# Unread products on TensorE in five waits of a two-block model kernel

## The chip, the core and the metric

The kernel runs on one core of a Trainium2 chip. The core has a matrix engine (TensorE, PE in the profile, with its weight loads as PEld), three engines for elementwise work (VectorE, DVE; ScalarE, ACT; GpSimd, POOL) and an engine that only issues transfers here (SyncE, SP). Each works through its own list of instructions in order; they meet by semaphores. The metric is the device time of one execution of the whole kernel in microseconds, median of several runs; lower is better.

## The reference

The kernel computes two blocks for one sequence of 256 tokens of width 1024, all in float32. The first block mixes by a gated delta rule and by dilated attention and has a layer of experts picked by product keys; the second is conditioned on a vector `c`, has a layer of sparse attention (NSA) and a layer of a gated linear recurrence, each followed by a mixture of experts. Only these parts are touched by the change:

```python
def gated_delta_rule(q, k, v, g, beta):          # chunks of tokens, 4 heads, 2 directions
    gcum = jnp.cumsum(g.reshape(r, n, c), axis=-1)
    decay = jnp.where(lower, jnp.exp(jnp.where(lower, diff, 0.0)), 0.0)
    kb = k * beta[..., None]
    lmat = jnp.where(strict, jnp.einsum('rnid,rnjd->rnij', kb, k) * decay, 0.0)
    amat = jnp.eye(c, dtype=jnp.float32) + lmat
    sol = lax.linalg.triangular_solve(amat, rhs, left_side=True, lower=True, unit_diagonal=True)
    ...
def deltanet_branch(q, k, v, z, a, b, conv_w, a_log, dt_bias, out_norm):
    ...
    o = rmsnorm(o, out_norm) * jax.nn.silu(z.reshape(bsz, s, DN_HEADS, DN_DV).astype(f32))
    ...
def nsa_mixer(h, rel_bias, w_in, q_gain, k_gain, cmp_pe, cmp_w1, cmp_w2, w_out):
    q, kc, vc, ks, vs, kw, vw, gl = jnp.split(h @ w_in, cuts, axis=-1)
    kc = rms_norm(compress_blocks(kc.reshape(kvs), cmp_pe[0], cmp_w1[0], cmp_w2[0]), k_gain[0])
    ...
        lg = jnp.einsum('bqgrd,bngd->bgrqn', q_b, kc) * scale + bias_tbl[:, :, t5_bucket_2(dist_c)]
        p_c = masked_softmax(lg, dist_c >= 0)          # compressed keys
        ...                                            # selected keys, window: p_s, p_w
        o = gate_b[..., 0:1] * o_c + gate_b[..., 1:2] * o_s + gate_b[..., 2:3] * o_w
```

## The kernel before

The program is a row of stages. Each opens its own tiles and semaphores, gives every engine a list of instructions written by hand, and ends with a barrier of all engines. A product of f32 operands appears in the trace as two records, a transpose as one.

`idle_products` (L133) issues n matmuls of the identity (128x128) with 512 columns of constants into a PSUM bank that nobody reads. The kernel has it in `norm_stage`, ahead of and behind the transposes (L499, L508), and in the mixture of experts (L2726, L2731).

`deltanet` (L907) treats four groups (two directions, two halves of the tokens) of four heads each. TensorE sums the gates and spreads them over rows (L1097 to L1100), transposes k and then v in four steps (L1101 to L1108), each of which VectorE copies out (L1002), and makes three groups of grams for each of the four groups (L1112 to L1123). Between them stand three blocks of `work`, an object of class `Conditioning` (L292), which multiplies a slice of the second block's conditioning matrix from the ring of weights by the vector (L334) while other engines are busy. VectorE turns the grams into a masked matrix in five steps (L1009 to L1017). Then a blocked triangular inverse runs in seven levels: GpSimd masks a block (L1084, and at the first level subtracts it from the identity, L1087), TensorE transposes or multiplies (`first`, L1129; `second`, L1145), ScalarE and VectorE copy and subtract. GpSimd's mask for step i waits for TensorE's product of step i-2, as two buffers alternate.

`head_norm_gate_turn` (L1200) is the next stage: TensorE does two or three blocks of conditioning, then eight transposes (L1251), VectorE copies them out (L1240), and the stage ends. The projection behind it (`project`, L524) takes its weights from the ring of three slots: the first block's products are plain f32 (L583), the later blocks are split in two parts by VectorE (L141, L146) and multiplied in three passes (L152 to L154).

`nsa_prepare` (L2045) transposes the inputs of the compression (L2195), does three slots of conditioning (`work.tensor(pe)`, behind L2200), of which the first is turned into columns once ScalarE has copied its row (L370, then L323), and then runs 64 records of compression products (L2209), which wait for the last row (`work.moved`, 3). ScalarE copies the first row only after its squares and root of the stage.

`nsa_attention` (L2228) flips the gates with a matrix that VectorE makes at the stage's start (L2356, L2451), scores the compressed keys in two groups (`c_score`: L2387, then the bias, L2392), scores the first two pairs of heads (`score`, L2413), turns the compressed probabilities (`c_turn`, L2401) once VectorE has shifted, and ScalarE and VectorE have scaled them, and then loops over 16 pairs: turn the probabilities (L2426), score the pair after next, multiply by the values (L2439, L2446). VectorE's row maximum of a pair is L2347.

## Time and profile before

| | us |
|---|---|
| median of 3 runs | 2287.07 |
| lowest and highest | 2286.28 and 2289.59 |
| the profiled execution: its time | 2286.01 |
| the profiled execution: span from first to last instruction | 2284.2 |

| engine | busy us | share of the span |
|---|---|---|
| TensorE | 2028.8 | 89% |
| VectorE | 1379.6 | 60% |
| ScalarE | 618.4 | 27% |
| GpSimd | 547.4 | 24% |

The mean granted clock of TensorE over the span is 0.975 of full speed. The clock has two levels here, 1.00 (2.4 GHz) and 0.50 (1.2 GHz); a value between them is a stretch with both. Ends of matmuls are modelled, and successive records overlap, so the pace of a group is read from the distance of starts rather than from the length of one record.

### The profile page before, as it was taken

Reading aid. Unit: us, or ns where it says so; the run is one execution under the profiler, and the core shown is the slowest. Engines: PE = TensorE matmul, PEld = TensorE weight load, DVE = VectorE, ACT = ScalarE, POOL = GpSimd, SP = SyncE. Lnnn points to the kernel's source line nnn. Section 1 sums busy time; section 2 is a strip of 40 time slices with the busy share of each in tenths; the row PEclk is TensorE's granted clock in tenths of the full one; section 3 lists DMA queues with packets and bytes.
Section 4 is the critical chain, followed back from the end, with each engine's and each line's share of the span. In section 5 each row is a group of like instructions: output and inputs, shape, how many; then the busy total and the mean of one; then the engine's idle time right before and its main releaser. Section 6 shows DMA issues by size and latency. Waiting matters only on the chain. (4 is left out here: it accounts for less than half of the span.)

```text
span 2284.2 us, 27579 instructions
## 1 busy us (share of the span) xinstructions
PE 2028.8 (89%) x10581; PEld 1341.9 (59%) x10581; DVE 1379.6 (60%) x2493; ACT 618.4 (27%) x1050; POOL 547.4 (24%) x499
## 2 busy tenths in 40 slices
PE   8889998997997777777779888999999979899998
PEld 7678897774542222222237765666775966566684
DVE  7255564557888888655665466433666764533494
ACT  2311103422111111000020262333652151433472
POOL 1032000104443333444320182000104252100000
PEclk9799999999999999999999799999999999999999
DMA  6830655639999999999965502998996533799897
GB/s 211 310 119 1 223 202 172 221 109 420 391 421 422 421 421 422 421 420 417 421 267 183 157 2 84 375 356 350 394 375 241 187 125 119 271 361 358 351 399 281
DMA packets 142431, 650.91 MB, mean 285 GB/s; under 512 B 17975, under 2 KB 22735, under 8 KB 97083
## 3 DMA queue, kind: packets, MB, share of 16 engines
q1 hardware_dynamic: 94012, 354.03, 41.1%
q0 software_dynamic: 46336, 291.93, 31.3%
q10 hardware_dynamic: 1952, 3.18, 0.4%
q8 instruction: 85, 1.39, 0.2%
q14 instruction: 46, 0.38, 0.0%
HBM read 642.40 MB, written 16.85 MB: 289 GB/s over the span
## 5 line engine op out<-in xcount | busy, mean ns | idle before, releaser
L1872 PE MATMUL psum<-peer_uv_rows,peer_weight_diagonal 128*128 128x512 f32 x932 | 453.5, 615 | 108.4 <-DVE peer_weight_diagonal L1998 108.0
L1872 PEld LDWEIGHTS psum<-peer_uv_rows,peer_weight_diagonal 128*128 128x128 f32 x932 | 161.7, 190 | 391.1 <-DVE peer_weight_diagonal L1998 266.2
L2005 DVE SCALAR_TENSOR_TENSOR peer_uv_rows<-peer_uv_rows,peer_x 128x1024 f32<-128x1024 f32 x233 | 285.6, 1226 | 145.4 <-DMA peer_uv_rows<-peer_uv,peer_index 143.2
L1826 POOL DMA_INDIRECT peer_uv_rows<-peer_uv,peer_index x233 | 241.7, 1037 | 446.9 <-PE psum L1872 330.2
L146 DVE TENSOR_TENSOR moe_weight_parts<-weight_ring,moe_weight_parts 128x2048 fp32r<-128x2048 f32 x80 | 182.6, 2291 | 155.0 <-ACT moe_weight_parts L2925 154.6
L1905 ACT ACTIVATE peer_gelu<-peer_dots 128x1 f32<-128x1 f32 x256 | 51.5, 202 | 552.1 <-DVE peer_uv_rows L2005 500.8
L2925 ACT ACTIVATE moe_weight_parts<-weight_ring 128x2048 fp32r<-128x2048 f32 x80 | 152.1, 1911 | 35.6 <-DMA weight_ring<-moe_w 24.4
L152 PE MATMUL psum<-moe_weight_parts,moe_block_x_parts 128*128 128x512 f32 x352 | 142.4, 404 | 10.5 <-DVE moe_weight_parts L146 5.7
L3044 POOL DMA_INDIRECT h_t<-moe_tokens,moe_block_tokens x30 | 34.8, 1159 | 450.6 <-PE psum L2743 410.0
L153 PE MATMUL psum<-moe_weight_parts,moe_block_x_parts 128*128 128x512 f32 x352 | 139.1, 395 | 0.0
L154 PE MATMUL psum<-moe_weight_parts,moe_block_x_parts 128*128 128x512 f32 x352 | 138.9, 395 | 0.0
L146 DVE TENSOR_TENSOR project_weight_parts<-weight_ring,project_weight_parts 128x2048 fp32r<-128x2048 f32 (+2 forms) x52 | 120.3, 2314 | 1.8
L2809 PE MATMUL psum<-weight_ring,moe_pair_x 128*64 128x512 f32 x384 | 117.7, 600 | 0.0
L141 DVE CAST project_weight_parts<-weight_ring 128x2048 fp32r<-128x2048 f32 (+2 forms) x52 | 68.6, 1319 | 50.0 <-PEq L574 31.2
L152 PE MATMUL psum<-project_weight_parts,project_x_parts 128*128 128x512 f32 (+2 forms) x256 | 97.4, 380 | 0.0
L154 PE MATMUL psum<-project_weight_parts,project_x_parts 128*128 128x512 f32 (+2 forms) x256 | 96.5, 377 | 0.0
L153 PE MATMUL psum<-project_weight_parts,project_x_parts 128*128 128x512 f32 (+2 forms) x256 | 96.5, 377 | 0.0
L152 PE MATMUL psum<-project_x_parts,project_weight_parts 128*128 128x256 f32 x320 | 91.1, 285 | 0.0
L154 PE MATMUL psum<-project_x_parts,project_weight_parts 128*128 128x256 f32 x320 | 90.5, 283 | 0.0
L153 PE MATMUL psum<-project_x_parts,project_weight_parts 128*128 128x256 f32 x320 | 90.5, 283 | 0.0
L1998 DVE TENSOR_SCALAR peer_weight_diagonal<-constants,peer_gelu,peer_gates 128x128 f32<-128x128 f32 x256 | 87.9, 344 | 2.4 <-ACT peer_gelu L1905 2.4
L152 PEld LDWEIGHTS psum<-moe_weight_parts,moe_block_x_parts 128*128 128x128 f32 x352 | 67.1, 191 | 34.8 <-DVE moe_weight_parts L146 11.7
(574 smaller groups left out, 3882.2 us busy)
## 6 DMA issues: line engine op xcount, KB each, us to landing
weight_ring<-moe_w SPq DMA_DIRECT2D x76, 2048.0 KB, 10.3
weight_ring<-ada_w SPq DMA_DIRECT2D x24, 2048.0 KB, 9.1
moe_weight_ring_end<-moe_w SPq DMA_DIRECT2D x20, 2048.0 KB, 12.6
weight_ring<-w_in SPq DMA_DIRECT2D x17, 2048.0 KB, 9.5
weight_ring<-hgrn_w_in SPq DMA_DIRECT2D x8, 2048.0 KB, 9.7
moe_results<-moe_block_out POOLq DMA_DIRECT2D x26, 512.0 KB, 10.5
weight_ring<-nsa_w_in SPq DMA_DIRECT2D x5, 2048.0 KB, 9.0
weight_ring<-peer_wq SPq DMA_DIRECT2D x4, 2048.0 KB, 8.1
```

What stands on the lines that cost most here:

```text
L141: return nc.vector.tensor_copy(out.bitcast(F32R), x)
L146: return eng.tensor_tensor(out.bitcast(F32R), x, high, ALU.subtract)
L152: nc.tensor.matmul(out, ll, rh, start=start, stop=False)
L153: nc.tensor.matmul(out, lh, rl, start=False, stop=False)
L154: return nc.tensor.matmul(out, lh, rh, start=False, stop=stop)
L1826: nc.gpsimd.indirect_dma_start(buffer(t), None, S.dram["peer_uv"], bass.IndirectOffsetOnAxis(ap=experts[:, t:t + 1], axis=0)).then_inc(row ...
L1872: last = nc.tensor.matmul(S.ps[:, 2 * a + c, :], diag[:, t % 4, :], v_rows(t)[:, c * BANK:(c + 1) * BANK], start=(i == 0), stop=(i == PICK ...
L1905: act.activation(act_of[:, t:t + 1], dots[:, t:t + 1], ACT.Gelu_apprx_tanh).then_inc(geared, 1)
L1998: nc.vector.tensor_scalar(diag[:, t % 4, :], S.cst[:, C_ID:C_ID + P], act_of[:, t:t + 1], gates[:, t:t + 1], ALU.mult, ALU.mult).then_inc( ...
L2005: nc.vector.scalar_tensor_tensor(u_rows(t), u_rows(t), 1.0, x2[:, t // PICKS, :], ALU.mult, ALU.mult, accum_out=dots[:, t:t + 1]).then_inc ...
L2809: last = nc.tensor.matmul(S.ps[half, LANES[2][w == "3"], :], xp[:, k, half], weights[side][:, k, :], start=(k == 0), stop=(k == KD - 1))
L2925: act.activation(wp[:, n % HALVES, 0, :].bitcast(F32R), raw_half(n), ACT.Copy).then_inc(high_made, 1)
```

## The change

Calls of `idle_products` are added in five places, and one call of the conditioning work is cut in two so that products can stand between its first slot and the others. Nothing is removed, and no value that is read changes.

- delta rule, opening: eight products into bank 7, behind the transposes of k and ahead of those of v
- delta rule, first level: 2, 1, 3 and 2 products ahead of the wait of each of the four groups' first product
- head norm: two products behind the last transposes
- sparse attention, preparation: four products between slot 0 and slots 1 and 2 of the conditioning
- sparse attention, opening: two products at its start, one behind each of the two groups of compressed scores, three ahead of each of the two turns of the compressed probabilities

```diff
@@ deltanet
                 for n in range(4):
+                    if n == 2:
+                        idle_products(S, 7, 8)
                     if n >= 2:
                         pe.wait_ge(s["turned_read"], n - 1)
@@ deltanet
                 def first(i):
                     n = i % 4
+                    if i < 4:
+                        idle_products(S, 7, (2, 1, 3, 2)[i])
                     pe.wait_ge(s["masked"], i + 1)
@@ head_norm_gate_turn
                     last.then_inc(turned, 1)
+                idle_products(S, 7, 2)
@@ nsa_prepare
-                work.tensor(pe)
+                work.tensor(pe, 0, 1)
+                idle_products(S, 6, 4)
+                work.tensor(pe, 1, 3)
                 pe.wait_ge(work.moved, 3)
@@ nsa_attention
+                idle_products(S, 5, 2)
                 pe.wait_ge(flip_made, 1)
@@ nsa_attention
                 for a in range(NT):
                     c_score(a)
+                    idle_products(S, 5, 1)
                 score(0)
                 score(1)
+                idle_products(S, 5, 3)
                 c_turn(0)
+                idle_products(S, 5, 3)
                 c_turn(1)
```

## Rows read from the trace of the kernel before

**Rows 1.** Page, parts 1 and 2: busy time by engine, granted clock by slice.

```profile
PE 2028.8 (89%) x10581; PEld 1341.9 (59%) x10581; DVE 1379.6 (60%) x2493; ACT 618.4 (27%) x1050; POOL 547.4 (24%) x499
...
PEclk9799999999999999999999799999999999999999
```

**Rows 2.** Timeline: start us, us, engine, line, tiles, count [idle before <-releaser]; existing products.

```profile
18.36 14.05 PE L583 MATMUL psum<-h_t,weight_ring 128*128 128x256 f32 x64 [0.30 <-PEq L410]
...
1418.21 5.40 PE L136 MATMUL psum<-constants 128*128 128x512 f32 x12
```

**Rows 3.** Stretches: busy us (count) of PE, PEld, DVE, ACT, POOL; PEclk, DMA, GB/s.

```profile
117.50:118.00 0.50, 0.00 (x0) 0.00 (x0) 0.50 (x2) 0.50 (x1) 0.00 (x0) 0.53 0.00 0
...
144.50:145.00 0.50, 0.00 (x0) 0.00 (x0) 0.00 (x0) 0.00 (x0) 0.48 (x1) 0.83 0.12 45
...
243.50:244.00 0.50, 0.33 (x1) 0.34 (x2) 0.00 (x0) 0.50 (x2) 0.35 (x1) 0.82 1.03 389
...
1314.00:1315.00 1.00, 0.59 (x3) 0.60 (x4) 0.95 (x2) 0.00 (x0) 0.00 (x0) 0.50 0.00 0
```

**Rows 4.** Timeline, delta rule's opening.

```profile
111.96 1.04 PE L1107 MATMUL psum<-constants,dn_k 128*128 128x128 f32 x8
118.07 1.97 PE L1107 MATMUL psum<-constants,dn_v 128*128 128x128 f32 x8 [5.08 <-DVE o_dn L1002]
...
123.78 0.69 DVE L1017 TENSOR_TENSOR delta_lmat<-delta_lmat,psum 128x512 f32<-128x512 f32 x1
...
125.27 1.13 PE L1092 MATMUL psum<-dn_q,dn_k 128*128 128x128 f32 x8 [0.18 <-PE psum L334]
```

**Rows 5.** Timeline, delta rule's first level.

```profile
140.69 1.09 PE L1139 MATMUL psum<-constants,delta_masked 128*128 128x128 f32 x8 [1.24 <-DVE delta_lmat L1017]
...
141.49 1.09 POOL L1084 TENSOR_TENSOR delta_masked<-delta_lmat,constants 128x512 f32<-128x512 f32 x1 [9.21 <-DVE delta_lmat L1017]
...
147.43 3.78 PE L1092 MATMUL psum<-delta_inverse,delta_masked 128*128 128x128 f32 x16 [1.28 <-POOL delta_masked L1084]
151.00 1.38 PE L1092 MATMUL psum<-delta_product,delta_inverse_t 128*128 128x128 f32 x8
...
153.11 1.06 PE L1092 MATMUL psum<-delta_inverse,delta_masked 128*128 128x128 f32 x8
```

**Rows 6.** Timeline, head norm's end and the projection behind it.

```profile
240.26 1.07 PE L1251 MATMUL psum<-constants,o_dn 128*128 128x128 f32 x8
243.67 15.77 PE L583 MATMUL psum<-h_t,weight_ring 128*128 128x256 f32 x64 [2.33 <-DMA weight_ring<-w_in]
...
253.78 2.29 DVE L146 TENSOR_TENSOR project_weight_parts<-weight_ring,project_weight_parts 128x2048 fp32r<-128x2048 f32 x1
```

**Rows 7.** Timeline of TensorE, sparse attention's preparation.

```profile
1260.29 4.02 PE L334 MATMUL psum<-weight_ring,cond 128*32 128x128 f32 x128
...
1267.62 0.43 PE L323 MATMUL psum<-constants,ada_row 128*128 128x4 f32 x2 [2.96 <-ACT ada_row L370]
1267.97 3.52 PE L334 MATMUL psum<-weight_ring,cond 128*32 128x128 f32 x64
...
1272.40 16.56 PE L2209 MATMUL psum<-nsa_prep_compress_in,nsa_prep_w 128*128 128x150 f32 x64 [0.56 <-ACT ada_row L370]
```

**Rows 8.** Timeline, sparse attention's opening.

```profile
1299.25 0.65 PE L2451 MATMUL psum<-nsa_x,nsa_attn_flip 128*128 128x48 f32 x4 [1.77 <-DVE nsa_attn_flip L2356]
1299.82 1.98 PE L2387 MATMUL psum<-nsa_kc_t,nsa_q_t 64*128 64x32 f32 x32
...
1302.74 3.63 PE L2387 MATMUL psum<-nsa_kc_t,nsa_q_t 64*128 64x32 f32 x32
...
1308.71 0.30 DVE L2347 CUSTOM_DVE_ANT_0 psum<-psum,nsa_hankel 128x128 f32<-128x128 f32 x1
...
1314.41 1.12 PE L2401 MATMUL psum<-constants,nsa_attn_probs_c 128*128 128x128 f32 x4 [2.02 <-DVE nsa_attn_probs_c L2333]
...
1317.58 0.30 DVE L2347 CUSTOM_DVE_ANT_0 psum<-psum,nsa_hankel 128x128 f32<-128x128 f32 x1 [0.46 <-PE psum L2413]
```

## The prediction

> **What bounds the kernel now.** I read the page first. TensorE is busy for 89% of the span and its granted clock is under nine tenths in two of the forty slices [rows 1]. So the whole kernel is close to bound by TensorE's order of work, and a change that only adds TensorE work must give it back through the clock. How much there is to give back is read from the stages that the change touches, with the timeline of the engines and with the granted clock in stretches of half a microsecond. In each of the five places the reader is to see the same pair: a wait of TensorE, and behind it products that take about twice the usual time because the clock went from 1.00 to 0.50 (2.4 to 1.2 GHz): delta rule's opening from 117.5 us, its first level from 144.9, the projection behind the head norm from 243.9 [rows 3], the second conditioning block in the sparse attention's preparation [rows 7] and the opening of the sparse attention itself [rows 8]. These stages hang on one another by a barrier at each stage's end, so time won or lost on TensorE's path in one of them moves all that follows. Behind the head norm the next long stretch is a projection, and TensorE is what it waits for there.
>
> **What an added product costs.** The change adds 8 + (2+1+3+2) + 2 + 4 + 10 = 32 products; each is one 128x512 f32 matmul, which the trace shows as two records. A call for six that the kernel already has gives twelve records, which take 5.40 us at full clock [rows 2]; less 0.59 for the last one's own length and over 11 steps that is 0.437 us a record, so 0.875 us a product. The 32 take 28 us, and nothing of it is read by anyone. The timeline has TensorE's records in the order of the program, so a product that is still running when the next needed operand arrives is pure delay. That they hold the clock is seen where the kernel already has them: after four records ahead of a projection, that projection's 64 records take 14.05 us [rows 2]; the same 64 records behind the head norm, where there are none, take 15.77 [rows 6].
>
> **Delta rule's opening: 0.35 us lost.** Eight products, 7.0 us, go between the transposes of k and those of v. The gap there is 5.08 us [rows 4]. The last k record starts at about 112.74, so the v transposes start at 112.85 + 7.0 = 119.85 instead of 118.07. At full clock they need 0.89 us to issue, so the grams start at 120.74, some 0.9 later than before; the grams' three groups and the 64 records of conditioning then take 0.89 x 3 + 1.75 (half of what such 64 take at half clock [rows 7]) and end near 125.2, about where they ended before, since before they began at half clock. But VectorE, which copies v before it builds the masked matrix, is 1.1 us later at first and ends its fifth step near 125.5 instead of 124.47 [rows 4]. TensorE's second group of grams waits for that step: 125.6 instead of 125.27. Everything up to the first level moves by these 0.35 us. Bounds: 1.8 lost (the whole overshoot) and 1.0 won (half of the low-clock work from 118.07 to 121, if VectorE turns out not to be late).
>
> **First level: 0.45 us lost.** The four groups of products run after TensorE's wait for the last gram to be read. At 140.69 the first two transposes were ready to go at once and GpSimd's chain hung on the first of them: its third mask starts at 141.49 [rows 5]. Two products ahead of that transpose (1.75 us) delay GpSimd by 1.75, and its masks and subtractions run end to end until the mask that releases TensorE at 147.43. That becomes 149.15; and two more products before the fourth transpose hold GpSimd's next mask until 149.75, so the second product of the level starts near 150.9, the group that began at 151.00 near 151.8, and the third product near 153.6, where it began at 153.11 [rows 5]. What pays for this is the clock: 16 records from 147.43 took 3.78 us where full clock needs 16 x 0.11 = 1.8, and the next eight 1.38 instead of 1.06. So 1.75 + 0.65 us of delay against some 2.1 us of clock, less small change: 0.45 lost. From 153 on TensorE runs without gaps in both kernels, so the loss stays. Bounds: 2.4 lost (nothing of the clock comes back), 1.5 won (the products fit into GpSimd's time).
>
> **Head norm: 1.7 us won.** Two products (1.75 us) follow the last transposes and run to about 242.9. The projection's first product waits until 243.67 for its weights by DMA [rows 6], so they lie under that wait; between the end of such products and the next stage's first matmul the trace has 0.3 us of idle time (the projection row of [rows 2]), which fits. The 64 records then take 14.05 instead of 15.77. The next block's weights, split on VectorE, are done at 253.78 + 2.29 = 256.07 [rows 6], before the new start of that block at about 257.4, so the gain isn't caught there. If the cover went (weights 0.8 us earlier), the products would cost that. Bounds: 0 and 2.0. The rows show full-rate transposes at a granted clock of 1.00 just before: 8 records in 1.07 us [rows 6], against four in 1.12 at 0.50 [rows 8].
> The Trainium skill ("TensorE: Matmul & The Clock Gate", Part 4: PE-mode transpose) speaks against part of this: it says that transpose-mode work does not count as busy in the same way and does not get the full clock. By that rule the transposes in the opening, the first level and the attention would gain nothing; the sum below would lose some 1.3 us (0.9 of v's transposes, 0.4 of the attention's) and come to about -1.0. The trace disagrees on the rate: the same kind of transpose took half the time at the higher clock.
>
> **Sparse attention's preparation: 1.2 us won.** `work.tensor` is cut in two: slot 0, TensorE's wait for it (its own product, about 0.25 us) with the ring slot given back earlier, four products (3.5 us), then slots 1 and 2. Before, slots 0 and 1 ran in one piece from 1260.29, then TensorE stood 2.96 us for ScalarE's first row, and slot 2 took 3.52 us at half clock [rows 7]. Now slot 0 ends near 1262.5, the products near 1266.1, slot 1 near 1268.2 with its bias, which is 0.55 us later than the row that TensorE waited for. Slot 2 at full clock needs 1.75 instead of 3.52. 0.55 - 1.77 = -1.2: the long chain of products that waited for the last row starts near 1271.2 instead of 1272.40 [rows 7]. The earlier release of the slot changes nothing, as SyncE's next weight load stands behind the sixteen Hankel loads in its queue. Bounds: 0.6 lost and 1.8 won.
>
> **Sparse attention's opening: 0.15 us won.** Ahead of the first softmax pass of VectorE (1308.71) go two products at the entrance, where only 0.35 us of their 1.75 fits before the flip matrix is made (+1.4), and one behind each of the two score groups (+1.75). Back come 1.65 us (the second group takes 3.63 us, the first 1.98 [rows 8]), 0.5 on the two bias groups and 0.6 on the scores: the pass starts 0.4 later. The next three lie under VectorE's scaling; the last three, 2.6 us into a wait of 2.02 [rows 8], end 0.8 late with the first delay, and c_turn, the turns and the next scores at full clock take that back, so that the third pass (1317.58), from which the loop runs in a fixed rhythm, starts near 1317.45. Bounds: 1.5 lost (only the entrance and the two single products count) and 1.5 won.
>
> **The sum.** +0.35 + 0.45 - 1.7 - 1.2 - 0.15 = -2.25 us. Against the profiled execution's 2286.01 us (span 2284.2 and 1.8 around it) that is 2283.8; the median of the runs, 2287.07, is 1.06 higher, so I forecast 2284.8.
>
> **Rivals.** (a) The gain is larger: the delta rule and the attention each win their upper bounds (1.0 + 1.5 + 1.5), because the products there are covered after all; with the other two that is -6.9, near 2280. For it: the low clock in the five places costs some 10 us in all. Against: the two starts that are pushed, 118.07 and 140.69, had their operands ready. 0.21. (b) The gain of the head norm is caught by the projection's split of weights or the next weights by DMA: -0.55, 2286.5. Against: the 1.3 us to spare at 256.07. 0.12. (c) The transposes keep their half rate: v's 1.97 us where full clock gives 1.06, and 0.4 of the attention's, so -1.0 and 2286.1. Against: the 8 records in 1.07 us. 0.03. (d) Slower: the products don't hold the clock in the opening, so it falls at 117.5 all the same. From there the last 2.7 products would cost twice as much, v's transposes would start at 122.2 (+4.1), the first level would pay its bound of 2.4, the attention's first four products would take 7.0 us, 6.6 of it ahead of the softmax pass, the preparation would pay 0.6 and the head norm win nothing: +13.7, 2301. It decides where the granted clock from 117.5 to 121 is 0.5 with the products in it. Against: the clock of 1.00 behind the existing ones. 0.04. The forecast itself: 0.60.
>
> **How the numbers follow.** About 0.2% (4.6 us) is what a measurement can tell from no change. Case (a) is faster, (d) slower; the forecast, (b) and (c) lie within, apart from the forecast's edges, 0.01 on either side. Faster 0.22, same 0.73, slower 0.05. The range reaches from (a) to just above no change, 2280.3 to 2288.0.
>
> **What would show it.** Right: granted clock 1.00 in all five places, the projection's 64 records near 14.1 us, the chain of products in the preparation 1.2 us nearer to its stage's start; v's transposes 1.8 us and the first transpose of the first level 1.75 us later behind what releases them. Wrong: a first level that ends earlier, or an attention loop that starts more than 1 us earlier against its stage's start.

## The result and the profile after

The changed kernel takes 2293.28 us (median of 20 runs, 2286.74 to 2301.04) beside 2287.27 for the kernel before on the same chip (20 runs). The ratio is 1.0024, 95% interval 1.0015 to 1.0032: about 6 us slower, where 2.25 us less was forecast. The profiled execution took 2294.54 us. From the page of the changed kernel (TensorE's and VectorE's busy time, the granted clock in forty slices, and the queue of instruction loads):

```profile
span 2292.8 us, 27707 instructions
PE 2046.6 (89%) x10645; PEld 1345.9 (59%) x10645; DVE 1380.1 (60%) x2493; ACT 618.3 (27%) x1050; POOL 544.3 (24%) x499
...
PEclk9799999999999999999999899999999999999999
...
q8 instruction: 85, 1.39, 0.3%
```

Against [rows 1] there are 128 instructions more (32 products of four: two weight loads and two matmuls), and the mean granted clock rose from 0.975 to 0.981. The clock was won and time was lost.

The timeline of TensorE in the changed kernel, in the edited places: opening, first level, head norm, preparation (start, length in us, line, operation, count, and in brackets the idle time before it and what ended it).

```profile
115.31 7.03 PE L136 MATMUL psum<-constants 128*128 128x512 f32 x16
122.18 1.04 PE L1109 MATMUL psum<-constants,dn_v 128*128 128x128 f32 x8
...
143.38 1.98 PE L136 MATMUL psum<-constants 128*128 128x512 f32 x4 [1.24 <-DVE delta_lmat L1017]
145.20 0.60 PE L1143 MATMUL psum<-constants,delta_masked 128*128 128x128 f32 x4
...
243.30 1.88 PE L136 MATMUL psum<-constants 128*128 128x512 f32 x4
246.25 14.08 PE L583 MATMUL psum<-h_t,weight_ring 128*128 128x256 f32 x64 [1.07 <-DMA weight_ring<-w_in]
...
1268.28 2.93 PE L334 MATMUL psum<-weight_ring,cond 128*32 128x128 f32 x64
1271.40 3.67 PE L136 MATMUL psum<-constants 128*128 128x512 f32 x8 [0.19 <-PE psum L334]
1275.00 1.95 PE L334 MATMUL psum<-weight_ring,cond 128*32 128x128 f32 x64
```

These answer to [rows 4] to [rows 7], and they look as forecast: v's transposes behind 7.03 us of products and in 1.04 us, the projection's 64 records in 14.08 us instead of 15.77. In stretches, the changed kernel's granted clock is as follows (busy us and count of each engine, then PEclk, DMA share, GB/s; the first two rows hold the delta rule's opening and first level, and the head norm):

```profile
115.00:159.00 44.00, 41.33 (x411) 31.91 (x410) 25.74 (x43) 5.88 (x14) 15.53 (x13) 1.00 0.44 160
234.00:264.00 30.00, 27.19 (x308) 23.57 (x307) 19.32 (x16) 7.08 (x13) 4.66 (x2) 1.00 0.65 228
347.00:382.00 35.00, 29.56 (x333) 24.91 (x332) 10.89 (x22) 7.85 (x16) 0.00 (x0) 0.90 0.72 234
```

The third row is a stage that nobody edited, the dilated attention, and there the clock is 0.90. Its timeline shows why; first the changed kernel, then the kernel before.

```profile
355.83 1.95 PE L334 MATMUL psum<-weight_ring,cond 128*32 128x128 f32 x64
357.72 0.41 PE L342 MATMUL psum<-ada_gate_bias,constants 32*32 32x128 f32 x5
362.47 0.63 PE L342 MATMUL psum<-ada_gate_bias,constants 32*32 32x128 f32 x3 [4.35 <-issue]
363.25 5.46 PE L1307 MATMUL psum<-ak,aq 128*128 128x256 f32 x12
```

```profile
354.92 1.95 PE L334 MATMUL psum<-weight_ring,cond 128*32 128x128 f32 x64
356.80 0.42 PE L342 MATMUL psum<-ada_gate_bias,constants 32*32 32x128 f32 x8
357.40 2.83 PE L1302 MATMUL psum<-ak,aq 128*128 128x256 f32 x12 [0.18 <-PE psum L342]
```

Eight small matmuls stood in one piece. Now five of them run, TensorE stands 4.35 us and waits for nothing that the trace shows ("issue"), and the other three follow. Behind the stop the clock is at its lower level and the twelve score records take 5.46 us instead of 2.83. By stretches of 2 us in the changed kernel (same columns):

```profile
359.00:361.00 2.00, 0.00 (x0) 0.00 (x0) 0.00 (x0) 0.00 (x0) 0.00 (x0) 1.00 1.05 387
361.00:363.00 2.00, 0.53 (x3) 0.18 (x2) 0.00 (x0) 0.00 (x0) 0.00 (x0) 0.85 0.56 202
363.00:365.00 2.00, 1.85 (x5) 1.50 (x5) 0.00 (x0) 1.31 (x2) 0.00 (x0) 0.50 0.11 31
```

From 359 to 361 no engine does anything; only the DMA engines are busy, at 387 GB/s, with the twelve loads of the Hankel rows (192 KB each).

To place the difference, the start of each record of TensorE is taken in both traces, the added products left out; the table gives how much later each stretch of the program made the changed kernel against the trace of before. The second column is a second trace of the changed kernel (after_again, below).

| stretch (us of before) | changed | changed, second trace | forecast |
|---|---|---|---|
| up to the delta rule, no edit | +2.4 | +0.3 | 0 |
| opening | +0.21 | +0.21 | +0.35 |
| first level | +0.54 | +0.53 | +0.45 |
| 230 to 240, no edit | -1.1 | -1.1 | 0 |
| head norm and projection | -1.2 | -1.5 | -1.7 |
| dilated attention, no edit | **+5.3** | **+4.6** | 0 |
| 368 to the preparation, no edit | +1.7 | +0.4 | 0 |
| preparation, from its products to L2209 | +0.1 | -0.5 | -1.2 |
| then to the attention, no edit | +1.6 | 0.0 | 0 |
| attention, to 1350 | +0.1 | +0.1 | -0.15 |
| rest, no edit | -1.2 | -0.8 | 0 |
| sum | +8.5 | +2.4 | -2.25 |

The edited stages are within 1.3 us of the forecast each. What repeats and was not forecast is the dilated attention, and the gain at 236 us.

### The profile page after: what moved, and what is told of

Same layout as the page of the kernel before. It is cut to its first block and busy times, and to the rows that moved or that the text cites. A ratio compares the mean times of both kernels' runs of the same rounds, so it can differ in the third digit from the quotient of the medians.

```text
span 2292.8 us, 27707 instructions
## 1 busy us (share of the span) xinstructions
PE 2046.6 (89%) x10645; PEld 1345.9 (59%) x10645; DVE 1380.1 (60%) x2493; ACT 618.3 (27%) x1050; POOL 544.3 (24%) x499
## 3 DMA queue, kind: packets, MB, share of 16 engines
q8 instruction: 85, 1.39, 0.3%
## 5 line engine op out<-in xcount | busy, mean ns | idle before, releaser
L136 PE MATMUL psum<-constants 128*128 128x512 f32 x152 | 75.8, 636 | 17.7 <-PEq L410 6.3
## 6 DMA issues: line engine op xcount, KB each, us to landing
moe_weight_ring_end<-moe_w SPq DMA_DIRECT2D x20, 2048.0 KB, 12.1
```

What stands on the lines that cost most here:

```text
L136: S.nc.tensor.matmul(S.ps[:, bank, :], S.cst[:, C_ID:C_ID + P], S.cst[:, 0:BANK], start=True, stop=True)
```

## What stops TensorE: the theories

**Theory F.** TensorE's instructions are loaded in blocks by a DMA queue of their own (q8: 85 packets, 1.39 MB, so 16384 B each; at 85 packets for 21290 matmuls and weight loads and a few hundred others that is 256 instructions of 64 B). A block's packet is usually seen when TensorE is 150 to 215 records past the start of the block before (three quarters of all packets in these traces). This is counted from the trace: records of TensorE's queue, waits for semaphores included, up to the packet, less 256 for each packet ahead of it. Where the count starts is arbitrary, so only its differences mean something. In the dilated attention the packet comes late, as it stands beside the Hankel loads. The DMA view of the changed kernel has no packet of q8 from 340 to 360 us, and from 360 to 361 this:

```profile
q1 hardware_dynamic: 211, 0.29, 77.7%
q10 hardware_dynamic: 67, 0.09, 23.5%
q8 instruction: 1, 0.02, 6.1%
```

It begins at 360.25, and TensorE resumes at 362.47. By 360.25 TensorE had run 449 records of its block and had no more; in the kernel before, the packet came at 359.53, just as late, but 72 instructions fewer had been run up to any point of the stage, so that it stood at 405 and never stopped. The Trainium skill ("Runtime: NRT & Kernel Launch", Instruction fetch mechanics) has the same unit, 16 KiB blocks of 256 instructions fetched by a DMA queue of the sequencer's own, and calls the cost of crossing a boundary mostly hidden. The trace agrees on the block and not on the cost here, 4.35 us and the clock behind it.

**Rivals.** The stop follows from a delay in the delta rule or the head norm; it is a wait for ScalarE or for weights that the trace misses; the products cost their own time on an engine that is 89% busy. In some expectations below stands a theory G as well: that some executions pay a second cost beside the stop, with the sparse attention's opening as its suspected place.

## Experiments

The kernel before was run beside each: 2287.98 us median in the first four, 2287.7 in the next four, 2288.54 in the third four, 2287.59 in the last three.

### The number of instructions without the change

**pad72**: the kernel before, with 72 instructions that do hardly anything, where TensorE waits for v.

```diff
                 for n in range(4):
+                    if n == 2:
+                        tiny_products(S, 7, 18)      # 128x4 columns each
                     if n >= 2:
                         pe.wait_ge(s["turned_read"], n - 1)
```

> The kernel before with 18 tiny products (128x4, 72 instructions) in the wait ahead of v's transposes in the delta rule's opening and nothing else; the wait there is 5.08 us and the products need some 2 to 4. They move TensorE's instruction stream by as many instructions as the change does ahead of the dilated attention. Theory F (fetch of instructions: the stream is loaded in blocks, the block that falls beside the Hankel loads of the dilated attention comes too late, and TensorE stands there for 4.35 us): the stop appears, with low clock behind it, and the time is 4 to 6 us over before (ratio 1.002). Theory L (the loss is made in the edited stages by products ahead of useful work; the stop was chance of one execution): no stop, time within 1 us of before.

Measured: 2294.77 us, ratio 1.0035 (1.0020 to 1.0050). The waits of TensorE from 344 to 372 us (us in total, times, longest):

```profile
PE psum L348 <- issue: 4.9, 1, 4.9
PE psum L340 <- PEq L561: 0.9, 1, 0.9
```

The stop is there with no product of the change, the packet at 449 records, and the stage loses 5.6 us.

**start72**: the same 72 instructions at the very start of the program, on a tile of ones that GpSimd writes, while TensorE waits for its first rows.

```diff
             def _(pe):
+                pe.wait_ge(ones_made, 1)
+                for _ in range(18):
+                    nc.tensor.matmul(S.ps[:, 5, 0:4], ones[:, :], ones[:, 0:4], start=True, stop=True)
                 pe.wait_ge(cst_in, 16)
```

> The kernel before with 18 products of four columns (72 instructions, as many as the change puts ahead of the dilated attention) at the very start of TensorE's list, on a tile that GpSimd fills, while TensorE waits 8.9 us for its first rows. No edited stage is touched. Theory F (late load of TensorE's instructions beside the Hankel loads): the stop of 4 to 5 us at L342 as in the changed kernel, the load landing 449 instructions into its block; the short stop of 0.9 us at 236 us of the kernel before is gone; 2291 to 2294. Rival (the stop comes from a delay in the delta rule or the head norm): no stop, 2288.

Measured: 2296.89 us, 1.0037 (1.0024 to 1.0050), 3 us over the range that I gave. The eighteen products end before the rows arrive (the first real record is 0.2 us later), no stage behind them is changed, and the timeline of the dilated attention reads:

```profile
357.06 0.41 PE L351 MATMUL psum<-ada_gate_bias,constants 32*32 32x128 f32 x5
362.18 0.63 PE L351 MATMUL psum<-ada_gate_bias,constants 32*32 32x128 f32 x3 [4.71 <-issue]
362.95 5.33 PE L1311 MATMUL psum<-ak,aq 128*128 128x256 f32 x12
```

The stop falls between the fifth and the sixth of the same eight records as in the changed kernel. 350 us lie between the cause and the place, and nothing but the count connects them. The stage loses 5.5 us; the first rival falls.

### Parts of the change

**mix_only** keeps the edits of `deltanet` and `head_norm_gate_turn` (72 instructions), **nsa_only** those of the two sparse stages (56, all behind the dilated attention).

```diff
mix_only:
+                        idle_products(S, 7, 8)
+                        idle_products(S, 7, (2, 1, 3, 2)[i])
+                idle_products(S, 7, 2)
nsa_only:
+                work.tensor(pe, 0, 1)
+                idle_products(S, 6, 4)
+                work.tensor(pe, 1, 3)
...
+                idle_products(S, 5, 2)
...
```

> Only the parts of the change in the delta rule and the head norm. Theory F: the stop in the dilated attention is there, time 4 to 6 us over before. Theory L: the delta rule's loss of 1.3 us less the head norm's gain of 1.7, so within 1 us of before, or 2 to 3 over if the delta rule loses more.

> Only the sparse attention's parts of the change (preparation and opening); nothing ahead of the dilated attention differs from before. Theory F: no stop there, time between 1 us under and 1.5 us over before. Theory L: a part of the loss stays, 2 to 4 us over before.

Measured: mix_only 2295.02 us, 1.0027 (1.0017 to 1.0037); its wait from 344 to 372 us is the line below. nsa_only 2289.01, 1.0005 (0.9996 to 1.0014), with no such line.

```profile
PE psum L342 <- issue: 4.8, 1, 4.8
```

The whole loss sits with the parts ahead of the dilated attention. mix_only comes into the stage 1.6 us earlier than before (head norm, and the stop at 236 us that is gone) and leaves it 4.1 later.

**open_only** and **first_only** keep eight products each, 32 instructions: the opening's, the first level's.

```diff
open_only:
+                    if n == 2:
+                        idle_products(S, 7, 8)
first_only:
+                    if i < 4:
+                        idle_products(S, 7, (2, 1, 3, 2)[i])
```

> The kernel before with the eight products of the delta rule's opening alone, 32 instructions of TensorE. Theory F: 405 + 32 = 437 instructions into the block when the late load lands, just under the 449 at which TensorE stood still in three runs, so no stop of more than 1 us; the opening itself costs 0.35 to 0.5: 2288 to 2289. Rival (the stop in the dilated attention follows from the opening's products themselves, whatever their number): a stop of 4 to 5 us, 2293.

> The kernel before with the eight products of the delta rule's first level alone, 32 instructions of TensorE. Theory F: as with the opening's eight, 437 instructions, no stop of more than 1 us; the level itself costs 0.45 to 0.8: 2288.3 to 2289. Rival (the first level's products set off the stop): 2293.

Measured: 2289.42, 1.0011 (1.0002 to 1.0021), and 2287.89, 1.0005 (0.9996 to 1.0013). The packets begin at 360.28 with TensorE at 439 records, and at 361.61 at 437: just short of 449. TensorE runs its last ten or twelve records and then stands there too, but only for a moment: 0.4 us in open_only, by its waits from 344 to 372 us,

```profile
PE psum L1331 <- issue: 0.4, 1, 0.4
```

and 0.3 us on the weight loads in first_only. Their steps in the traces are +0.21 for the opening and +0.54 for the first level, as in the changed kernel. Two halves of about nothing make a whole of 5 us, which no sum of parts gives.

**head_prep** keeps the head norm's two products and the preparation's four (8 instructions ahead of the dilated attention).

```diff
+                idle_products(S, 7, 2)          # head_norm_gate_turn
-                work.tensor(pe)                 # nsa_prepare
+                work.tensor(pe, 0, 1)
+                idle_products(S, 6, 4)
+                work.tensor(pe, 1, 3)
```

> The kernel before with two parts of the change: the two products behind the head norm's transposes, and the four in the sparse attention's preparation. It adds 8 instructions of TensorE ahead of the dilated attention, 24 in all. Theory F: the late load of instructions finds TensorE some 413 instructions into the block, so no stop; -1.7 from the head norm and 0 to -1.2 from the preparation: 2285 to 2286.5 beside 2288. Rival (each unread product costs its time on a TensorE that is busy for 89%): 2288 to 2290.

Measured: 2289.51 us, 1.0004 (0.9992 to 1.0016). No stop (415 records). The time lies in the rival's range, not in that of theory F. The trace has 0.9 us of gain from 240 to 262 us and 0.4 in the preparation, so the products don't cost their time there, but the median doesn't show the gain: one of this size is not resolved by these runs.

**att_only** keeps the ten products of the sparse attention's opening.

```diff
+                idle_products(S, 5, 2)
                 pe.wait_ge(flip_made, 1)
...
+                    idle_products(S, 5, 1)
...
+                idle_products(S, 5, 3)
                 c_turn(0)
+                idle_products(S, 5, 3)
```

> The kernel before with the ten products of the sparse attention's opening alone. No instruction is added ahead of the dilated attention, so theory F wants no stop there. Theory G with its place in the attention's opening: two heaps of times, one near 2287 at 0.976 to 0.978, one near 2292 at 0.973, and a low-clock stretch near 1301 us in a trace of the second. If the opening's products cost nothing in any execution: one heap, 2286.5 to 2288.5.

Measured: 2288.54 us beside 2288.54, 1.0003 (0.9995 to 1.0012). The ten products cost nothing and bring nothing; the second score group takes 1.97 us in this trace, no longer 3.63 [rows 8], and the attention's loop is 0.1 us later all the same. That doesn't yet settle theory G: eight of the twelve times lie from 2285.4 to 2289.9, four from 2292.3 to 2292.8, and the trace (2288.4) is one of the first eight.

### Moving the loads, not the instructions

**hank_late**: the changed kernel with all its products; the Hankel loads begin only when two of the stage's three conditioning rows are made.

```diff
             def _(sp):
+                sp.wait_ge(work.made, 2)
                 for h in range(NH):
-                    for g in range(2):
+                    for g in range(3):
                         load_hankel(S, sp, hank[:, g * NH + h, :], g * NH + h, hank_in[h])
...
             def _(act):
-                for h in range(NH):
-                    load_hankel(S, act, hank[:, 2 * NH + h, :], 2 * NH + h, hank_in[h])
```

> The changed kernel with its 32 products, but the twelve loads of the Hankel rows of the dilated attention are all issued by SyncE, and only once TensorE has made the second of the stage's three conditioning rows (about 355 us, not 351). Theory F (the load of TensorE's next 16384 B of instructions, asked for near 353 us, queues behind those twelve loads, so that TensorE runs dry): the instruction packet lands within 2 us of 353, the stop of 4.35 us at L342 is gone, the low clock behind it too; against that VectorE's first row maximum waits some 3 us longer for its Hankel rows, so the stage ends about 2 to 3 us earlier than in the changed kernel and the time is 2290 to 2292. Rival 1 (the stop is set by the number of instructions alone, whatever the transfers): the stop stays, 2293 or more. Rival 2 (the stop is a wait for ScalarE or for the weights that the trace misses): it stays, 2293 or more.

Measured: 2292.4 us, 1.0020 (1.0010 to 1.0030), so by its time this kernel is not clear of the changed one; the profiled execution took 2287.75. The DMA view from 353.5 to 355 us holds one packet and nothing else, and TensorE's timeline is whole again:

```profile
q8 instruction: 1, 0.02, 4.9%
```

```profile
357.16 0.42 PE L342 MATMUL psum<-ada_gate_bias,constants 32*32 32x128 f32 x8
357.76 2.83 PE L1308 MATMUL psum<-ak,aq 128*128 128x256 f32 x12 [0.18 <-PE psum L342]
363.91 0.33 PE L1335 MATMUL psum<-constants,dilated_probs 128*128 128x128 f32 x1 [3.32 <-ACT dilated_probs L1351]
```

With the same instructions at the same places and only the loads moved, the packet begins at 354.25, six microseconds earlier, at 277 records; the stop and the low clock are gone (scores in 2.83 us). What is late next is VectorE's first row maximum, which waits for the Hankel rows until 361.81, so the stage still loses 1.0 us. The second rival falls, and so does the thought that the number alone decides: number and traffic together do.

**after_again** and **hank_late_again** are the same two kernels once more, each for a second trace.

> The changed kernel once more, for a second trace of it. Theory F (late load of instructions): the stop of 4 to 5 us at L342 stands in this trace too, with the instruction packet near 360 us, 449 instructions into its block; median near 2293. Theory G (a second cost that only some executions pay, since the times of the changed kernel lie in two heaps, near 2288 at a mean granted clock of 0.982 and near 2294 at 0.979): a trace at 0.979 or less has a low-clock stretch of 10 us or more that the trace at 0.981 lacked, most likely in the sparse attention's opening near 1301 us.

> The changed kernel with the dilated attention's twelve Hankel loads held back, once more: its eleven times lay in two heaps, 2286.5 to 2288.9 at a mean granted clock of 0.981 to 0.982 (its trace was one of these), and 2291.9 to 2295 at 0.977 to 0.981. Theory F alone: no stop at L342, 2288 to 2289 in the trace whatever the clock. Theory G: a trace at 0.980 or less shows no stop at L342 either, but a low-clock stretch of 10 us or more elsewhere, and is 4 to 6 us longer.

Measured: after_again 2295.14 us, 1.0033 (1.0021 to 1.0046), stop at the same record (below), packet at 357.7 and 449 records. hank_late_again 2289.82, 1.0005 (0.9996 to 1.0014), no stop, stage +1.9.

```profile
PE psum L342 <- issue: 4.3, 1, 4.3
```

Neither trace has a long low-clock stretch at 1301 us: that guess of theory G fell here. hank_late_again grew by 4.3 us between 1335 and 1990, behind the last edit, with low-clock stretches that were 6.83 and 13.65 us where the trace of before has 3.41 and 6.83; hank_late, the same kernel, grew by 0.6 there. Over the sixteen other traces the part of the program behind 1350 us moved by -1.9 to +5.6 us against that of before. At least the 3.7 us between two traces of one kernel are scatter between executions, and such scatter makes the times lie apart.

**hank_no_att** is hank_late without the ten products of the attention.

```diff
 (hank_late)
-                idle_products(S, 5, 2)
-                    idle_products(S, 5, 1)
-                idle_products(S, 5, 3)
-                idle_products(S, 5, 3)
```

> The changed kernel without the ten products of the sparse attention's opening, and with the twelve Hankel loads held back. Theory G with its place in the attention's opening (its products run at half clock in some executions, and there cost up to 6 us): one heap of times, 2287 to 2290, at 0.975 to 0.978. If the second heap comes from elsewhere: two heaps as before, median 2291 to 2293.

Measured: 2290.88 us (2287.01 to 2297.64), 1.0010 (0.9998 to 1.0021). The times are spread as before, so the spread does not come from the attention's products: this, more than att_only, speaks against the place that theory G names.

### Moving the block's boundary

**all_pad256** adds 46 small products (184 instructions) to the changed kernel, between the conditioning slots ahead of the delta rule (36) and ahead of its right-hand sides (10). With the change's own 72 the stream is shifted by one whole block of 256 at the dilated attention.

```diff
-                work.tensor(pe, 2, 6)
+                work.tensor(pe, 2, 3)
+                tiny_products(S, 0, 18)
+                work.tensor(pe, 3, 4)
+                tiny_products(S, 0, 18)
+                work.tensor(pe, 4, 6)
...
+                tiny_products(S, 7, 10)
                 for n in range(4):
                     pe.wait_ge(s["rhs_ready"], n + 1)
```

> The changed kernel with 46 tiny products (184 instructions) more, 36 of them in two waits for conditioning weights ahead of the delta rule and 10 in a wait behind its last level, so that the stream stands in the dilated attention where it stood before, one whole block later (72 + 184 = 256 instructions). Theory F: no stop in the dilated attention, time some 5 us under the changed kernel, within 1 to 2 us of before. Theory L: the stop has nothing to do with it, time as the changed kernel, 6 us over before, or a little more.

Measured: 2295.78 us, 1.0038 (1.0024 to 1.0051). No stop (386 records), but the padding has its own price: a group of the view by lines, from 60 to 112 us,

```profile
L142 PE MATMUL psum<-constants 128*128 128x4 f32 x72 | 10.0, 276 | 0.0
```

10.0 us of which the wait for weights there covered 5.4, and the trace falls 7 us behind from 84 to 100 us and another 3.6 around the ten products. I had expected a time within 1 to 2 us of the kernel before; it is 7.8 over. The run shows the stop gone and can't show what that is worth.

**start128** and **start128_after** put 32 such products at the program's start, in the kernel before and in the changed one.

```diff
+                for _ in range(32):
+                    nc.tensor.matmul(S.ps[:, 5, 0:4], ones[:, :], ones[:, 0:4], start=True, stop=True)
```

> The kernel before with 32 such products (128 instructions) at the start. Theory F: the block's load is then asked for before the Hankel loads begin at 351 us, so it lands in time and there is no stop: 2287 to 2289, with up to 1 us for the products that outlast the wait at the start. Theory H (a shift of the instruction blocks costs some 2 us in stretches behind the dilated attention, which would be the part of the changed kernel's loss that its traces don't show): 2290 to 2292.

> The changed kernel with the same 32 products at the start: with its own 128 instructions it is one whole block of 256 behind the sparse attention, so that all later blocks begin where they do in the kernel before, and the load in the dilated attention is asked for near 347 us, ahead of the Hankel loads. Theory F: no stop at L342; by the stages' own steps in the traces (+0.2 opening, +0.5 first level, -1.1 at 236 us, -1.5 head norm, -0.3 preparation, +0.1 sparse attention, up to +1 at the start) 2286 to 2288. Rival (the products cost time of their own in executions that no trace caught): 2290 to 2293, as in the changed kernel with its Hankel loads held back.

Measured: start128 2301.86 us, 1.0060 (1.0046 to 1.0074), start128_after 2297.89, 1.0045 (1.0031 to 1.0058). Both pay more at the start than I expected, the 64 records taking 13.8 us, so that all that follows is 5.8 us later:

```profile
1.00 13.82 PE L292 MATMUL psum<-setup_ones 128*128 128x4 f32 x64 [1.00 <-POOL setup_ones L270]
```

Less these 5.8, start128 is 8.5 us over the kernel before, though no stage is edited, and start128_after 4.5. My expectation for start128 was wrong: the load is still late, TensorE again runs dry at 449 records, now earlier in the stage, and stands 2.4 us ("PE psum L343 <- issue" in its waits). start128_after has its packet at 396 records and no stop at L342, and its dilated attention loses nothing (-0.2); one of its conditioning products waits 0.9 us ("issue"), it too the first behind 449 records. So the stop depends on where in the stage the block runs out: a shift of 8 or 32 instructions is harmless, 72 costs 5.3, 128 costs 2.2, 200 costs nothing.

All traces together, by the records TensorE had run of its block when the packet came:

| kernel | records | stop, us | stage, us |
|---|---|---|---|
| before | 405 | none | 0 |
| att_only, nsa_only | 405, 407 | none | -0.1, +0.1 |
| head_prep | 415 | none | +0.1 |
| first_only, open_only | 437, 439 | 0.3, 0.4 at L1331 | -0.1, +0.2 |
| changed, after_again | 449, 449 | 4.35, 4.3 | +5.3, +4.6 |
| pad72, mix_only, start72 | 449 each | 4.9, 4.8, 4.7 | +5.6, +5.7, +5.5 |
| start128 | 449 | 2.4 | +2.2 |
| all_pad256, start128_after | 386, 396 | none, 0.9 at L343 | -1.5, -0.2 |
| hank_late, hank_late_again, hank_no_att | on time: 277, 277, 280 | none | +1.0, +1.9, +1.9 |

One number holds for all of them. In twelve of the seventeen traces TensorE stands once with nothing to wait for and a late packet ahead of it (in before, att_only and nsa_only at 237 to 239 us, in the others in the dilated attention), each time behind exactly 449 records, and each time it starts again 2.2 to 2.5 us after the packet's beginning. How long it stands, 0.3 to 4.9 us, is set by how long ahead of the packet it got through them.

## Why the prediction was wrong, point by point

**The step that failed** is the sum itself: "+0.35 + 0.45 - 1.7 - 1.2 - 0.15". It has terms for the edited stages alone, as if a product that ends in its stage had no effect behind it but time. Every product is also four instructions of TensorE's stream, and the 18 ahead of the dilated attention moved a block's end by 72 instructions. That cost 5.3 us at a place 115 us behind the last of them. Rival (d), the only one on the slower side, named another mechanism (the clock falls in the opening all the same), and that did not happen: the granted clock is 1.00 from 115 to 159.

Could it be seen beforehand? The page of before lists q8, and its trace has the same packet at 359.53 us, as late as in the changed kernel, with TensorE 44 records from standing still. It even has a small stop of the kind, 2.4 us behind a packet that came at 375 records (234.44):

```profile
236.84 0.27 PE L323 MATMUL psum<-constants,ada_row 128*128 128x4 f32 x1 [0.94 <-issue]
```

That record, too, is the first behind 449. This stop is gone in every trace of a kernel with instructions added ahead of it and stays in att_only and nsa_only, which have none: -1.1 us, the same cause with the other sign, and not forecast either. It is gone in head_prep as well, whose products all stand behind it: there the packet came at 271 records, so a stop this short also depends on the execution.

**Opening**, +0.35 forecast: +0.21, but not on the way forecast. The block of conditioning ahead of the second group of grams starts at 125.83 (123.14 before), which is the whole 0.21 once the 2.48 us are taken off by which the trace was late already; and the group follows that block with the same 0.18 us of idle time as in [rows 4]. So the loss came over TensorE's own records; VectorE's fifth step does not show as what released them, and that the size came near is in part luck. First the kernel before, then the changed one:

```profile
123.14 1.95 PE L334 MATMUL psum<-weight_ring,cond 128*32 128x128 f32 x64
...
125.83 1.95 PE L334 MATMUL psum<-weight_ring,cond 128*32 128x128 f32 x64
127.96 1.13 PE L1092 MATMUL psum<-dn_q,dn_k 128*128 128x128 f32 x8 [0.18 <-PE psum L334]
```

**First level**, +0.45: +0.54; the first transpose came 1.8 us later behind its release, as forecast. **Head norm**, -1.7: -1.2 and -1.5. The 64 records took 14.08 us as said, and the products lie under the wait with 1.07 us to spare; what is missing came from the weights, which landed 0.2 to 0.5 us later in these two traces.

**Preparation**, -1.2: +0.1 and -0.5, -0.3 to -0.4 in six other traces with this edit, and -1.3 in all_pad256, where the low clock ended ahead of slot 0. The term that was mis-sized is "slot 0 ends near 1262.5", 2.2 us behind its start. Slot 0 and its gap took 3.1 us (1268.28 to 1271.40), since the low clock that comes in from the stage before reached 2 us into it here and only 0.7 in the trace of before. Its length differs between traces of kernels that don't edit anything ahead of it (6.83 or 10.24 us), so one trace was too little to rest 0.9 us on. The same holds for the measurement: from slot 0 to L2209 the eight traces without this edit take 12.0 to 13.4 us, that of before 12.1, and the nine with it 11.1 to 12.1. On the mean the edit gains 1.0 us; the trace of before, against which forecast and table count, was one of the quickest.

**Attention**, -0.15: +0.1. Against the stage's entry VectorE's first softmax pass starts 0.8 us later, where 0.4 was forecast, and the third 0.1 later, where 0.13 earlier was forecast. TensorE's records are up to 0.7 us ahead at that point, and the loop's first turns give it back.

**Rival (c)** had the transposes at half rate: v's eight records took 1.04 us at 1.00, so it did not occur. The Trainium skill ("TensorE: Matmul & The Clock Gate", Part 4: PE-mode transpose) has such a rule, and this case's traces disagree with it. **Rival (b)** did not occur: the projection kept its gain.

By their own steps the edits sum to about -0.8 us, with the gain at 236 us to -1.9, and the stop turns that into +2.7 to +3.4. The medians say +6.0 and +6.6. The kernels with the full stop lie 6.0 to 9.3 us over the kernel before, those without it 0 to 4.7 (the padding of all_pad256 and of the program's start left out), so the stop accounts for most of the loss. **What stays open** is a remainder of some 3 us: kernels without the long stop (hank_late +4.7 and +1.3, hank_no_att +2.3, open_only +1.7, head_prep +1.8, start128_after +4.5 after its start) are slower than their steps. No one place of their traces holds it. That a shift of the instruction stream costs time by itself in untouched stages is not shown: start128, in which no stage is edited, loses 2.3 us between 121 and 165 us to longer low-clock stretches, but nsa_only, with nothing added ahead of 1260 us, loses 2.1 there in the same way. Part of the remainder may lie in the measure: all steps are counted against one trace of the kernel before, and that execution (2286.01) was 1.3 us under the median. No version here beat the kernel before beyond its interval.

## What to carry to other kernels

Count the instructions that an edit adds to an engine's stream as well as their time: a block of them is loaded by DMA, and where that load falls beside a burst of other transfers, some tens of instructions more, hundreds of microseconds earlier, can stop the engine. In the trace this is an idle time put down to "issue", here often in the middle of a run of equal records, with a packet of the instruction queue 2.2 to 2.5 us ahead of its end; look for late packets before the edit, and for how many records were left. Filling a wait to hold the clock is worth something only where TensorE's pace behind the wait sets the end: here clearly so at one place of five, the head norm, and on the mean of the traces in the preparation.

## What the runs showed of the hardware

- TensorE stood still behind 449 records of a block in twelve traces; an instruction packet that mostly comes at 150 to 215 records came at 386 to 449 beside twelve loads of 192 KB.
- From the late packet's beginning to work took 2.2 us in the changed kernel (360.25 to 362.47) and 2.2 to 2.5 in all twelve; after the stop of 4.35 us the granted clock was 0.50 for 6.8 us (3.4 in after_again).
- A product of four columns is not free: at the program's start 64 records took 13.8 us, 0.22 us each, at a granted clock of 1.00.
